# Block sums of the inner rows: made once by VectorE and kept in DRAM scratch instead of summed by GpSimd beside every product

## The chip, the cores and the metric

The kernel runs on one core of one Trainium2 chip. The metric is the device time of the whole program in microseconds (us), as the median of several executions. The five engines are named as the profile names them: PE (TensorE, matrix products), DVE (VectorE), ACT (ScalarE), POOL (GpSimd), and SP (SyncE), which here only issues DMAs, one after the other, in the order of its program.

## The reference, cut to what matters

The reference is one inference step of a two-layer encoder for 1024 prompt tokens and 128 sample tokens, 1152 rows in all. Layer 0 has latent attention and layer 1 a chunked gating mixer. Each is followed by the part that the change is about, a squared-ReLU feed-forward of width 4096 on rows of 1024:

```
def sq_relu_ffn(h, w1, w2):
    return jnp.square(jax.nn.relu(h @ w1)) @ w2

f_p = sq_relu_ffn(modulated_norm(x_p, norm2_g[i], sh2_p, sc2_p), ffn_w1[i], ffn_w2[i])
x_p = x_p + gt2_p[:, None, :] * f_p
```

The matrices are float32. The kernel writes each as hi + lo, two halves that PE can multiply at its fast rate, and makes every product from three (hi·hi, lo·hi, hi·lo): L110, L111 and L112 of the helper `mm3`.

## The kernel before, in words

In each layer the feed-forward has two stages, and both multiply 2x2 blocks with seven products P1 to P7 in place of eight. That needs sums of blocks on both sides: S1, S2, S3, S4 of the one, T1 to T4 of the other.

**The first product** (h @ w1) runs over 16 pairs of 128 hidden channels; a `Pair` is one step. PE makes P1, P5, P6, P2, P7, P4, P3 in this order (`H_ORDER`), each for two groups of tokens. Per pair:
- SP loads the w1 of the next pair (`load_w1`, tiles w0q or w1q by turns).
- POOL makes its four block sums (`w1_sums`).
- ACT and DVE split it: ACT copies the hi half, DVE subtracts for the lo half (`w1_lo_q`, `w1_lo_r`).
- ACT copies P1, P6 and P7 out of PSUM; DVE adds what is left (`read_hidden` C11, C22, C12) into two tiles, piece 0 and piece 1 of 128 x 1152. P3 lies in the PSUM bank of P5, so it waits until C22 has been read.
- DVE squares both pieces (`square`), and SP stores them to the DRAM scratch `hid`.

The 14 pairs between the first and the last are a loop on every engine.

**The second product** (hidden @ w2) runs over 8 slabs of 512 channels, and in each over 4 steps of 256 tokens (32 steps n in a layer), and ends with a product for the sample tokens. In a step PE makes P1, P5, P6, P2, P7, P3, P4. The rows of the hidden matrix come back from DRAM (`load_s`, three tiles by turns, s0, s1, s2). Before the change POOL makes their block sums (`s_sums`: s0q in place, then three into s0r). ACT then copies the hi halves (`s_hi_q`, `s_hi_r`) and DVE subtracts (`s_lo_q`, `s_lo_r`). w2 has its sums and splits on DVE and ACT. ACT copies three products of a step out of PSUM into `tmp`, POOL adds these to the accumulator (`add`), and DVE adds the other four from PSUM (`read`).

Nothing is scheduled by a planner. Each engine runs its rows in the order in which the program is written, with semaphores between them, so one late wait holds up all rows behind it on that engine.

## Time and profile before

| | us |
|---|---|
| median of 3 runs | 2893.41 (2891.55 to 2895.07) |
| the profiled execution, its own time | 2895.44 |
| its span in the trace | 2893.8 |
| PE busy | 2676.5 (92% of the span) |
| DVE busy | 1812.8 (63%) |
| POOL busy | 1183.7 (41%) |
| ACT busy | 1146.9 (40%) |

The busy times are averages over stages with different limits. The first product takes 1000 to 1337 us of the trace in layer 0 and 2145 to 2480 in layer 1, the second product 1340 to 1739 and 2482 to 2883. Ahead of the first product lies the output projection of the mixer, from about 870 and from about 2010. PEclk is the granted TensorE clock, 1.00 for 2.4 GHz and 0.50 for 1.2 GHz.

### The profile page before, as it was taken

Reading aid. Unit: us, or ns where it says so; the run is one execution under the profiler, and the core shown is the slowest. Engines: PE = TensorE matmul, PEld = TensorE weight load, DVE = VectorE, ACT = ScalarE, POOL = GpSimd, SP = SyncE. Lnnn points to the kernel's source line nnn. Section 1 sums busy time; section 2 is a strip of 40 time slices with the busy share of each in tenths; the row PEclk is TensorE's granted clock in tenths of the full one; section 3 lists DMA queues with packets and bytes.
Section 4 is the critical chain, followed back from the end, with each engine's and each line's share of the span. In section 5 each row is a group of like instructions: output and inputs, shape, how many; then the busy total and the mean of one; then the engine's idle time right before and its main releaser. Section 6 shows DMA issues by size and latency. Waiting matters only on the chain.

```text
span 2893.8 us, 45017 instructions
## 1 busy us (share of the span) xinstructions
PE 2676.5 (92%) x16628; PEld 2360.4 (82%) x16628; DVE 1812.8 (63%) x2502; ACT 1146.9 (40%) x2330; POOL 1183.7 (41%) x1022
## 2 busy tenths in 40 slices
PE   6989999899999899999998988999979999998987
PEld 4877878799988799998776766888879999776766
DVE  4577787655566734437888885224673344878886
ACT  3355555345453322224343433223332322444342
POOL 1122102166543322224788871000332222588886
PEclk9999999899999999999999998999999999999999
DMA  6244434322244222233322355125323222432325
GB/s 238 70 163 142 158 109 149 120 67 67 72 147 148 88 93 92 108 108 131 101 85 77 109 146 150 44 66 179 125 79 115 93 92 99 139 102 76 110 77 98
DMA packets 161007, 320.59 MB, mean 111 GB/s; under 512 B 15604, under 2 KB 105876, under 8 KB 157528
## 3 DMA queue, kind: packets, MB, share of 16 engines
q1 hardware_dynamic: 157352, 305.69, 31.6%
q0 software_dynamic: 3504, 12.91, 2.3%
q8 instruction: 92, 1.51, 0.2%
q14 instruction: 59, 0.48, 0.0%
HBM read 249.34 MB, written 69.21 MB: 110 GB/s over the span
## 4 chain that ended last, share of the span: by engine, by line
PE 43%; DVE 15%; issue 7%; POOL 3%; ACT 1%; DMA 1%; SPq 0%; DVEq 0%; POOLq 0%; ACTq 0%
PE psum L110 14%; PE psum L112 14%; PE psum L111 14%; DVE half_acc L3227 3%; DVE half_s0r_lo L3199 1%; DVE half_s1q_lo L3194 1%; DVE half_s_lo L3203 1%; DVE half_s2r_lo L3199 1%; DVE half_s1r_lo L3199 1%; DVE half_s0q_lo L3194 1%; PE psum L3575 0%; DVE half_w1q_lo L3183 0%; DMA gate_w_raw<-in_cm_w_in 0%; DVE half_w2q_lo L3183 0%; DVE half_w0q_lo L3183 0%
## 5 line engine op out<-in xcount | busy, mean ns | idle before, releaser
L2938 POOL TENSOR_TENSOR half_acc<-half_acc,half_tmp 128x512 f32<-128x512 f32 x176 | 309.2, 1810 | 129.7 <-ACT half_tmp L2674 88.8
L2674 ACT ACTIVATE half_tmp<-psum 128x512 f32<-128x512 f32 x176 | 104.4, 593 | 295.5 <-PE psum L112 293.4
L3227 DVE TENSOR_TENSOR half_acc<-half_acc,psum 128x512 f32<-128x512 f32 x240 | 161.4, 678 | 85.0 <-PE psum L112 82.8
L3103 DVE TENSOR_TENSOR half_piece<-psum,half_snap_p 128x576 f32<-128x576 f32 (+1 forms) x34 | 24.5, 721 | 297.9 <-PE psum L112 297.9
L2569 ACT ACTIVATE half_snap_u<-psum 128x288 f32<-128x288 f32 x128 | 52.6, 411 | 282.6 <-PE psum L112 282.6
L110 PE MATMUL psum<-half_h_hi,half_w0q_hi 128*128 128x288 f32 x512 | 154.0, 301 | 6.9 <-DVE half_h_lo L3068 4.5
L111 PE MATMUL psum<-half_h_lo,half_w0q_hi 128*128 128x288 f32 x512 | 152.2, 297 | 0.0
L110 PE MATMUL psum<-half_h_hi,half_w1q_hi 128*128 128x288 f32 x512 | 151.8, 297 | 0.1
L112 PE MATMUL psum<-half_h_hi,half_w0q_lo 128*128 128x288 f32 x512 | 151.7, 296 | 0.0
L111 PE MATMUL psum<-half_h_lo,half_w1q_hi 128*128 128x288 f32 x512 | 151.0, 295 | 0.0
L112 PE MATMUL psum<-half_h_hi,half_w1q_lo 128*128 128x288 f32 x512 | 150.5, 294 | 0.0
L110 PE MATMUL psum<-gate_w_hi,gate_hT_hi 128*128 128x512 f32 x288 | 116.4, 404 | 11.2 <-issue 6.0
L2875 POOL TENSOR_TENSOR half_w0q_raw<-half_w0q_raw 128x512 f32<-128x512 f32 x16 | 20.7, 1295 | 254.2 <-DMA half_w0q_raw<-in_w 254.2
L110 PE MATMUL psum<-half_h_hi,half_w0r_hi 128*128 128x288 f32 x384 | 114.9, 299 | 8.9 <-issue 4.3
L110 PE MATMUL psum<-half_w_hi,half_m_hi 128*128 128x512 f32 x288 | 115.3, 400 | 4.9 <-DVE half_w_lo L1724 3.0
L110 PE MATMUL psum<-half_h_hi,half_w1r_hi 128*128 128x288 f32 x384 | 114.6, 298 | 4.5 <-DVE half_piece L3103 4.5
L2875 POOL TENSOR_TENSOR half_w1q_raw<-half_w1q_raw 128x512 f32<-128x512 f32 x16 | 21.5, 1347 | 236.4 <-DMA half_w1q_raw<-in_w 236.4
L111 PE MATMUL psum<-half_h_lo,half_w1r_hi 128*128 128x288 f32 x384 | 113.9, 297 | 0.0
L111 PE MATMUL psum<-half_h_lo,half_w0r_hi 128*128 128x288 f32 x384 | 113.9, 297 | 0.0
L112 PE MATMUL psum<-gate_w_hi,gate_hT_lo 128*128 128x512 f32 x288 | 113.9, 395 | 0.0
L111 PE MATMUL psum<-gate_w_lo,gate_hT_hi 128*128 128x512 f32 x288 | 113.8, 395 | 0.0
L112 PE MATMUL psum<-half_h_hi,half_w1r_lo 128*128 128x288 f32 x384 | 113.6, 296 | 0.0
(750 smaller groups left out, 9485.0 us busy)
## 6 DMA issues: line engine op xcount, KB each, us to landing
scratch_hid<-half_piece SPq DMA_DIRECT2D x64, 576.0 KB, 3.1
patt_mod_w<-in_ada_w_ffn SPq DMA_DIRECT2D x32, 768.0 KB
half_w0q_raw<-in_w SPq DMA_DIRECT2D x24, 1024.0 KB, 5.8
half_w1q_raw<-in_w SPq DMA_DIRECT2D x24, 1024.0 KB, 5.8
patt_mod_w<-in_ada_w_att SPq DMA_DIRECT2D x16, 1024.0 KB, 5.0
half_s0q_raw<-scratch_hid SPq DMA_DIRECT2D x22, 512.0 KB, 3.7
half_s1q_raw<-scratch_hid SPq DMA_DIRECT2D x22, 512.0 KB, 3.7
half_s2q_raw<-scratch_hid SPq DMA_DIRECT2D x20, 512.0 KB
```

Source lines behind the costliest of these rows:

```text
L110: pe.matmul(out, a_hi, b_hi, start=first, stop=False, skip_group_check=go_on)
L111: pe.matmul(out, a_hi, b_lo, start=False, stop=False, skip_group_check=go_on)
L112: return pe.matmul(out, a_lo, b_hi, start=False, stop=last, skip_group_check=go_on)
L2569: act.activation(out[:, grp, :], psum[:, bank(product, grp), 0:GN], ACT.Copy).then_inc(a.c.snap, 1)
L2674: act.activation(out, psum[:, o_bank_of(product, j), :], ACT.Copy).then_inc(a.c.taken, 1)
L2875: pool.tensor_tensor(q[:, S3, :], q[:, A21, :], q[:, A11, :], ALU.subtract).then_inc(a.c.w1_sum, 1)
L2938: pool.tensor_tensor(part, part, a.tmp[(3 * n + m) % 4][:], ALU.add).then_inc(a.c.added, 1 if i % SLABS else 3)
L3103: dve.tensor_tensor(a.piece[i.par][f_][:, cols, side, :], psum[:, b:b + len(grps), 0:GN], snap[:, cols, :], ALU.add).then_inc(a.c.hid_read, 1)
L3194: dve.tensor_tensor(a.s_qlo[r][:], a.s_q[r][:], f(a.s_qhi[r][:]), ALU.subtract).then_inc(a.c.s_ready, 1)
L3199: dve.tensor_tensor(a.s_rlo[r][:], a.s_r[r][:], f(a.s_rhi[r][:]), ALU.subtract).then_inc(a.c.s_ready, 1)
L3203: dve.tensor_tensor(a.s8_lo[:], a.s8[:], f(a.s8_hi[:]), ALU.subtract).then_inc(a.c.s8_ready, 1)
L3227: dve.tensor_tensor(part, part, of, ALU.add).then_inc(a.c.read, 1)
```

## The change

- DVE makes the block sums of the hidden rows (S3 in place in piece 0, S2, S1, S4, and one for the sample tokens) once per pair, in `block_sums`. SP stores them to new DRAM scratch (`hid_sums`, `hid_8`), and `load_s` and `load_s8` load them beside the rows. `s_sums` and `s8_sum` of POOL are gone.
- The two squares of a pair and its block sums stand at the head of the next pair on DVE (`finish_rows`); those of the last pair stand in the first step of the second product.
- In the second product the sums and splits of the next slab's w2 are placed otherwise over the four steps, on ACT and DVE, and the split of the next rows stands ahead of the read of C11.
- Ahead of the first product the sums and lo halves of h that POOL made (`h_sums`, `h_lo`) go to DVE, and the first pair takes its second group in the same order as its first.
- Where layer 0 ends, the splits of the next weights stand a little earlier.

The diff, cut to its core:

```
@@ -2305,9 +2318,23 @@
                              ).then_inc(a.c.w1_in[par], 16)
 
             def store_piece(a, i, f):
-                sp.wait_ge(a.c.sq_ready, i.count(2, 2 - f))
+                if f == 1:
+                    sp.wait_ge(a.c.sq_ready, i.count(2, 1))
+                else:
+                    sp.wait_ge(a.c.sum_ready, i.count(N_SUM, 1))
                 sp.dma_start(hid[i.index(2, f)], a.piece[i.par][f][:].rearrange("p a b n -> p (a b n)")
                              ).then_inc(a.c.piece_stored[i.par][f], 16)
+
+            def store_sums(a, i):
+                sp.wait_ge(a.c.sum_ready, i.count(N_SUM, N_SUM))
+                for place, s in enumerate((S1, S2, S4)):
+                    sp.dma_start(hid_sums[i.index(1, 0)][:, :, place, :], a.sums[s][:]).then_inc(a.c.sums_stored, 16)
+                sp.dma_start(hid_8[i.index(1, 0)], a.sum8[:]).then_inc(a.c.sums_stored, 16)
+
+            def store_pair(a, i):
+                store_piece(a, i, 1)
+                store_piece(a, i, 0)
+                store_sums(a, i)
 
             def load_w2(a, i, e):
                 u = w2_unit(i, e)
...
@@ -2328,9 +2356,12 @@
                 r = s_place(a, n)[0]
                 sp.dma_start(a.s_q[r][:].rearrange("p e f n -> p (e f) n"),
                              hid_slabs[i % SLABS, :, :, 2 * j * P:2 * (j + 1) * P]).then_inc(a.c.s_in[r], 16)
+                sp.dma_start(a.s_r[r][:].rearrange("p e r n -> p e (r n)"), hid_sum_slabs[i % SLABS, j]
+                             ).then_inc(a.c.s_in[r], 16)
 
             def load_s8(a, i):
                 sp.dma_start(a.s8[:, 0:4, :], hid_slabs[i % SLABS, :, :, SEQ:]).then_inc(a.c.s8_in, 16)
...
@@ -2361,44 +2392,44 @@
                     sp.sem_inc(a.c.piece_stored[1][f], 16)
 
             def hidden_steps(a):
-                store_piece(a, Pair(a, 0), 1)
-                store_piece(a, Pair(a, 0), 0)
+                store_pair(a, Pair(a, 0))
                 with sp.Fori(0, FFS // 2 - 1) as m:
                     for i in (Pair(a, 1, m), Pair(a, 2, m)):
                         sp.wait_ge(a.c.hid_ready, i.count(UNITS))
                         load_w1(a, i, 1)
-                        store_piece(a, i, 1)
-                        store_piece(a, i, 0)
+                        store_pair(a, i)
                 i = Pair(a, FFS - 1)
                 sp.wait_ge(a.c.hid_ready, i.count(UNITS))
                 slab = SLABS * a.layer
                 load_w2(a, slab, 0)
-                sp.wait_ge(a.c.hid_ready, unit_done(i, P5, 1))
+                sp.wait_ge(a.c.hid_ready, unit_done(i, P5, 0))
                 load_w2(a, slab, 1)
                 for n, product in enumerate((P6, P2, P7)):
                     sp.wait_ge(a.c.hid_ready, unit_done(i, product, 1))
                     load_s(a, PAIRS * slab + n)
-                store_piece(a, i, 1)
-                store_piece(a, i, 0)
                 sp.wait_ge(a.c.hid_ready, i.count(UNITS, UNITS))
                 sp.wait_ge(a.c.hid_read, hid_reads(i, 3))
                 load_s8(a, slab)
+                load_w2(a, slab + 1, 0)
+                load_w2(a, slab + 1, 1)
+                store_pair(a, i)
 
             def output_steps(a):
                 for i in slabs_of(a):
                     if i % SLABS:
                         sp.wait_ge(a.c.f_ready, i * N_JOBS)
-                        load_s8(a, i)
-                    if i % SLABS < LAST:
+                    if 0 < i % SLABS < LAST:
                         load_w2(a, i + 1, 0)
                         load_w2(a, i + 1, 1)
-                    else:
+                    if i % SLABS == LAST:
...
@@ -2642,17 +2674,17 @@
                 w2_hi_r(a, i, e)
 
             def s_hi_q(a, n):
-                act.wait_ge(a.c.s_sum, 4 * n + 1)
+                act.wait_ge(a.c.s_in[s_place(a, n)[0]], s_place(a, n)[1])
                 r = s_place(a, n)[0]
                 act.activation(a.s_qhi[r][:], a.s_q[r][:], ACT.Copy).then_inc(a.c.s_hi_ready, 1)
 
             def s_hi_r(a, n):
-                act.wait_ge(a.c.s_sum, 4 * n + 4)
+                act.wait_ge(a.c.s_in[s_place(a, n)[0]], s_place(a, n)[1])
                 r = s_place(a, n)[0]
...
@@ -2879,54 +2915,12 @@
-            def s_sums(a, n):
-                ring, loaded = s_place(a, n)
-                q, r = a.s_q[ring], a.s_r[ring]
-                s1, s2, s4 = (r[:, :, s - 4, :] for s in (S1, S2, S4))
-                x11, x12, x21, x22 = (s_slots(q, s) for s in (A11, A12, A21, A22))
-                pool.wait_ge(a.c.s_in[ring], loaded)
-                pool.tensor_tensor(x21, x21, x11, ALU.subtract).then_inc(a.c.s_sum, 1)
-                pool.wait_ge(a.c.s_sum, 4 * n + 1)
-                pool.tensor_tensor(s2, x21, x22, ALU.add).then_inc(a.c.s_sum, 1)
-                pool.wait_ge(a.c.s_sum, 4 * n + 2)
-                pool.tensor_tensor(s1, s2, x11, ALU.add).then_inc(a.c.s_sum, 1)
-                pool.tensor_tensor(s4, x12, s2, ALU.subtract).then_inc(a.c.s_sum, 1)
-
-            def s8_sum(a, i):
-                pool.wait_ge(a.c.s8_in, 16 * (i + 1))
-                x = a.s8[:, 0:4, :].rearrange("p (e f) n -> p e f n", f=2)
-                pool.tensor_tensor(a.s8[:, 4:6, :], x[:, :, 0, :], x[:, :, 1, :], ALU.add).then_inc(a.c.s8_sum, 1)
...
@@ -2947,22 +2941,12 @@
-                    if n % STEPS + 2 < STEPS:
-                        s_sums(a, n + 2)
-                    if j == 0:
-                        s8_sum(a, i)
...
@@ -3105,36 +3096,53 @@
 
             def square(a, i, f_):
                 if f_ == 1:
-                    dve.wait_ge(a.c.c21_ready, c21_takes(i, 2 if i.first else 1))
-                dve.wait_ge(a.c.hid_read, hid_reads(i, (6 if i.first else 3) if f_ == 0 else (5 if i.first else 2)))
+                    dve.wait_ge(a.c.c21_ready, c21_takes(i, 1))
+                dve.wait_ge(a.c.hid_read, hid_reads(i, 3 if f_ == 0 else 2))
                 x = a.piece[i.par][f_][:]
                 dve.scalar_tensor_tensor(x, x, 0.0, x, ALU.max, ALU.mult).then_inc(a.c.sq_ready, 1)
 
-            def hidden_step(a, i):
+            def block_sums(a, i):
+                dve.wait_ge(a.c.sq_ready, i.count(2, 2))
+                dve.wait_ge(a.c.sums_stored, i.count(64, 1))
+                flat = [a.piece[i.par][f_][:].rearrange("p a b n -> p (a b n)") for f_ in range(2)]
+                x11, x12, x21, x22 = (flat[f_][:, 0:SEQ].rearrange("p (j s n) -> p j s n", s=2, n=P)[:, :, side, :]
+                                      for side in range(2) for f_ in range(2))
+                s1, s2, s4 = (a.sums[s][:] for s in (S1, S2, S4))
+                dve.tensor_tensor(x21, x21, x11, ALU.subtract).then_inc(a.c.sum_ready, 1)
+                dve.wait_ge(a.c.sum_ready, i.count(N_SUM, 1))
+                dve.tensor_tensor(s2, x21, x22, ALU.add).then_inc(a.c.sum_ready, 1)
+                dve.wait_ge(a.c.sum_ready, i.count(N_SUM, 2))
+                dve.tensor_tensor(s1, s2, x11, ALU.add).then_inc(a.c.sum_ready, 1)
+                dve.tensor_tensor(s4, x12, s2, ALU.subtract).then_inc(a.c.sum_ready, 1)
+                dve.tensor_tensor(a.sum8[:], flat[0][:, SEQ:], flat[1][:, SEQ:], ALU.add).then_inc(a.c.sum_ready, 1)
+
+            def finish_rows(a, i):
+                square(a, i, 1)
+                square(a, i, 0)
+                block_sums(a, i)
+
+            def hidden_step(a, i, before):
                 both = (0, 1)
+                finish_rows(a, before)
                 if i.last:
                     slab, n = SLABS * a.layer, STEPS * a.layer
                     w2_sums(a, slab, 0)
                     read_hidden(a, i, C11, both)
                     w2_lo_q(a, slab, 0)
                     read_hidden(a, i, C22, both)
+                    w2_lo_r(a, slab, 0)
                     w2_sums(a, slab, 1)
-                    w2_lo_r(a, slab, 0)
                     s_lo_q(a, n)
                     w2_lo_q(a, slab, 1)
                     read_hidden(a, i, C12, both)
                     s_lo_r(a, n)
                     w2_lo_r(a, slab, 1)
-                    square(a, i, 1)
-                    square(a, i, 0)
                     return
                 read_hidden(a, i, C11, both)
                 w1_lo_q(a, i, 1)
                 read_hidden(a, i, C22, both)
                 w1_lo_r(a, i, 1)
-                square(a, i, 1)
                 read_hidden(a, i, C12, both)
-                square(a, i, 0)
 
             def first_hidden(a):
                 i = Pair(a, 0)
...
@@ -3251,30 +3260,46 @@
                 for n in steps_of(a):
                     i, j = n // PAIRS, n % PAIRS
                     last, more = i % SLABS == LAST, (n + 1) % STEPS > 0
+                    fresh = i % SLABS == 0
+                    if not last and j == (2 if fresh else 1):
+                        w2_lo_q(a, i + 1, 0)
+                    if not last and not fresh and j == 2:
+                        w2_sums(a, i + 1, 1)
+                    if not last and j == 3:
+                        w2_lo_q(a, i + 1, 1)
+                    if fresh and j == 0:
+                        square(a, Pair(a, FFS - 1), 1)
+                        square(a, Pair(a, FFS - 1), 0)
                     read(a, n, C22)
-                    if not last and j >= 2:
-                        w2_lo_q(a, i + 1, j - 2)
+                    if fresh and j == 0:
+                        block_sums(a, Pair(a, FFS - 1))
+                    if more:
+                        s_lo_q(a, n + 1)
                     read(a, n, C11)
                     if more:
-                        s_lo_q(a, n + 1)
+                        s_lo_r(a, n + 1)
+                    if j == 1:
+                        s8_lo(a, i)
+                    if fresh and j == 1:
+                        w2_sums(a, i + 1, 1)
+                    if not last and j == 2:
+                        w2_lo_r(a, i + 1, 0)
                     if last:
                         extra(j, 0)
                     read(a, n, C12)
-                    if more:
-                        s_lo_r(a, n + 1)
+                    if not last and j == 0:
+                        w2_sums(a, i + 1, 0)
                     read(a, n, C21)
-                    if not last and j < 2:
-                        w2_sums(a, i + 1, j)
-                    if not last and j >= 2:
-                        w2_lo_r(a, i + 1, j - 2)
-                    if j == 1:
-                        s8_lo(a, i)
+                    if not last and j == 3:
+                        w2_lo_r(a, i + 1, 1)
                     if last:
+                        extra(j, 1)
                         scale(a, 2 * j)
                         scale(a, 2 * j + 1)
-                        extra(j, 1)
                     if j == PAIRS - 1:
                         read_8(a, i)
+                    if last:
+                        extra(j, 2)
                 scale(a, SAMPLE)
 
             def project_steps(a, start):
```

SP in the loop of the first product, before. Pieces 8448 and 8447 are pieces 1 and 0 of one pair, 8446 and 8445 of the next; `half_w1q_raw<-in_w` is `load_w1`.

```order
L2309 DMA scratch_hid<-half_piece_8447 128x1152
L2368 REGISTER_ALU
L2304 ISA
L2304 DMA half_w1q_raw<-in_w 128x2x1024
L2308 REGISTER_ALU
L2309 ISA
L2309 DMA scratch_hid<-half_piece_8446 128x1152
L2308 REGISTER_ALU
L2309 ISA
L2309 DMA scratch_hid<-half_piece_8445 128x1152
```

The same place in the changed kernel:

```order
L2325 DMA scratch_hid<-half_piece_8447 128x1152
...
L2331 DMA scratch_hid_sums<-half_sum_8449 512x1x128
L2331 ISA
L2331 DMA scratch_hid_sums<-half_sum_8450 512x1x128
L2331 ISA
L2331 DMA scratch_hid_sums<-half_sum_8451 512x1x128
L2332 ISA
L2332 DMA scratch_hid<-half_sum_8452 128x128
L2398 REGISTER_ALU
L2317 ISA
L2317 DMA half_w1q_raw<-in_w 128x2x1024
```

Between the store of piece 0 and the load of w1 stand four stores of sums now, and the first of them waits for the last sum that DVE makes of this pair.

DVE in the same loop, before: the rows from the lo half of one w1 to the reads of C11 and C22 of the pair behind it (L3103 is `read_hidden`, L3111 `square`).

```order
L3089 TENSOR_TENSOR half_w0r_lo<-half_w0r_raw,half_w0r_hi 128x1536
...
L3111 SCALAR_TENSOR_TENSOR half_piece_8448<-half_piece_8448 128x1152
...
L3103 TENSOR_TENSOR half_piece_8447<-psum,half_snap_u_8450 128x2x288
L3111 SCALAR_TENSOR_TENSOR half_piece_8447<-half_piece_8447 128x1152
...
L3103 TENSOR_TENSOR half_piece_8445<-psum,half_snap_p_8449 128x2x288
...
L3084 TENSOR_TENSOR half_w1q_lo<-half_w1q_raw,half_w1q_hi 128x2048
...
L3103 TENSOR_TENSOR half_piece_8446<-psum,half_snap_u_8451 128x2x288
```

The same stretch of the changed kernel (L3094 is `read_hidden`, L3102 `square`, L3111 to L3117 `block_sums`):

```order
L3094 TENSOR_TENSOR half_piece_8447<-psum,half_snap_u_8454 128x2x288
...
L3102 SCALAR_TENSOR_TENSOR half_piece_8448<-half_piece_8448 128x1152
L3102 SCALAR_TENSOR_TENSOR half_piece_8447<-half_piece_8447 128x1152
...
L3111 TENSOR_TENSOR half_piece_8447<-half_piece_8447 128x4x128
...
L3113 TENSOR_TENSOR half_sum_8450<-half_piece_8447,half_piece_8448 128x512
...
L3115 TENSOR_TENSOR half_sum_8449<-half_sum_8450,half_piece_8447 128x512
L3116 TENSOR_TENSOR half_sum_8451<-half_piece_8448,half_sum_8450 128x512
L3117 TENSOR_TENSOR half_sum_8452<-half_piece_8447,half_piece_8448 128x128
...
L3094 TENSOR_TENSOR half_piece_8445<-psum,half_snap_p_8453 128x2x288
...
L3075 TENSOR_TENSOR half_w1q_lo<-half_w1q_raw,half_w1q_hi 128x2048
...
L3094 TENSOR_TENSOR half_piece_8446<-psum,half_snap_u_8455 128x2x288
```

The square of piece 1 moved behind the read of C12, and the sums came in behind both squares. The order of C11, `w1_lo_q` and C22 is as it was.

POOL in the second product, before (L2938 is `add`, L2919 to L2924 `s_sums`):

```order
L2938 TENSOR_TENSOR half_acc_8473<-half_acc_8473,half_tmp_8483 128x512
L2938 TENSOR_TENSOR half_acc_8473<-half_acc_8473,half_tmp_8482 128x512
L2938 TENSOR_TENSOR half_acc_8474<-half_acc_8474,half_tmp_8484 128x512
L2919 TENSOR_TENSOR half_s0q_raw<-half_s0q_raw 128x2x128
L2921 TENSOR_TENSOR half_s0r_raw<-half_s0q_raw 128x2x128
L2923 TENSOR_TENSOR half_s0r_raw<-half_s0r_raw,half_s0q_raw 128x2x128
L2924 TENSOR_TENSOR half_s0r_raw<-half_s0q_raw,half_s0r_raw 128x2x128
```

And in the changed kernel, where L2932 is `add`:

```order
L2932 TENSOR_TENSOR half_acc_8477<-half_acc_8477,half_tmp_8487 128x512
L2932 TENSOR_TENSOR half_acc_8477<-half_acc_8477,half_tmp_8486 128x512
L2932 TENSOR_TENSOR half_acc_8478<-half_acc_8478,half_tmp_8488 128x512
L2932 TENSOR_TENSOR half_acc_8479<-half_acc_8479,half_tmp_8486 128x512
L2932 TENSOR_TENSOR half_acc_8479<-half_acc_8479,half_tmp_8489 128x512
L2932 TENSOR_TENSOR half_acc_8480<-half_acc_8480,half_tmp_8487 128x512
```

Between one step's adds and the next step's nothing is left on POOL.

## Rows read from the trace of the kernel before

**Rows 1.** Busy time by stretch: one pair, one slab; then chain rows three slabs apart.
```profile
1292.40:1314.80 22.40, 22.40 (x170) 22.40 (x169) 9.04 (x7) 6.38 (x10) 5.13 (x4) 1.00 0.28 99
1400.00:1449.80 49.80, 45.03 (x194) 35.54 (x193) 42.20 (x40) 21.23 (x27) 42.43 (x30) 1.00 0.28 90
...
1399.93 1.56 DVE half_s2r_lo L3199
...
1549.36 1.56 DVE half_s2r_lo L3199
```

**Rows 2.** Waits of PE, slab of 1400.0 to 1449.8: waiting line, releaser, total, times, longest.
```profile
PE psum L110 <- ACT half_tmp L2674: 1.7, 2, 1.1
...
PE psum L110 <- DVE half_s1q_lo L3194: 1.4, 1, 1.4
```

**Rows 3.** Groups by line and shape, same slab: busy us, mean ns, idle before.
```profile
L3194 DVE TENSOR_TENSOR half_s2q_lo<-half_s2q_raw,half_s2q_hi 128x1024 fp32r<-128x1024 f32 x1 | 2.3, 2280 | 1.5 <-POOL half_s2r_raw L2924 1.5
...
L3194 DVE TENSOR_TENSOR half_s1q_lo<-half_s1q_raw,half_s1q_hi 128x1024 fp32r<-128x1024 f32 x1 | 1.2, 1212 | 0.0
...
L2938 POOL TENSOR_TENSOR half_acc<-half_acc,half_tmp 128x512 f32<-128x512 f32 x13 | 22.8, 1772 | 6.7 <-DVE half_acc L3227 3.4 <-ACT half_tmp L2674 3.3
L2919 POOL TENSOR_TENSOR half_s0q_raw<-half_s0q_raw 128x256 f32<-128x256 f32 x2 | 3.7, 1853 | 0.0
```

**Rows 4.** Timeline of SP's queue, where one pair ends and the next begins: start, us, line.
```profile
1291.75 3.57 SPq L2309 DMA_DIRECT2D scratch_hid<-half_piece  x2
1295.58 0.41 SPq L2304 DMA_DIRECT2D half_w1q_raw<-in_w  x1
```

**Rows 5.** Timelines of POOL, DVE and PE in the pair from 1292.46 to 1314.86.
```profile
1301.29 1.29 POOL L2875 TENSOR_TENSOR half_w1q_raw<-half_w1q_raw 128x512 f32<-128x512 f32 x1 [16.77 <-DMA half_w1q_raw<-in_w]
...
1292.66 0.76 DVE L3103 TENSOR_TENSOR half_piece<-psum,half_snap_u 128x576 f32<-128x576 f32 x1 [1.08 <-PE psum L112]
1293.45 1.36 DVE L3111 SCALAR_TENSOR_TENSOR half_piece<-half_piece 128x1152 f32<-128x1152 f32 x1
...
1306.70 2.29 DVE L3084 TENSOR_TENSOR half_w1q_lo<-half_w1q_raw,half_w1q_hi 128x2048 fp32r<-128x2048 f32 x1 [0.48 <-POOL half_w1r_raw L2880]
1309.26 0.76 DVE L3103 TENSOR_TENSOR half_piece<-psum,half_snap_u 128x576 f32<-128x576 f32 x1 [0.27 <-ACT half_snap_u L2569]
...
1314.86 0.30 PE L110 MATMUL psum<-half_h_hi,half_w1q_hi 128*128 128x288 f32 x1
```

**Rows 6.** Timeline of DVE: the first and the last of four 128x512 sums in a row.
```profile
1323.89 0.69 DVE L3172 TENSOR_TENSOR half_w0r_raw<-half_w0q_raw 128x512 f32<-128x512 f32 x1 [6.68 <-DMA half_w0q_raw<-in_w]
...
1325.95 0.69 DVE L3177 TENSOR_TENSOR half_w0r_raw<-half_w0q_raw,half_w0r_raw 128x512 f32<-128x512 f32 x1
```

**Rows 7.** Layer 0, second pair: SP, POOL, PE timelines; busy time and clock of a stretch.
```profile
1002.84 0.40 SPq L2304 DMA_DIRECT2D half_w0q_raw<-in_w  x1
...
1010.42 1.31 POOL L2875 TENSOR_TENSOR half_w0q_raw<-half_w0q_raw 128x512 f32<-128x512 f32 x1 [22.73 <-DMA half_w0q_raw<-in_w]
...
1018.86 0.40 PE L110 MATMUL psum<-half_h_hi,half_w1r_hi 128*128 128x288 f32 x1 [2.23 <-DVE half_piece L3103]
...
1023.67 0.29 PE L110 MATMUL psum<-half_h_hi,half_w0q_hi 128*128 128x288 f32 x1
...
1020.00:1023.00 3.00, 3.00 (x15) 3.00 (x14) 1.74 (x2) 0.00 (x0) 0.00 (x0) 0.50 0.11 42
```

**Rows 8.** Layer 1, second pair: timeline of PE, and busy time and clock behind it.
```profile
2163.91 0.40 PE L110 MATMUL psum<-half_h_hi,half_w1r_hi 128*128 128x288 f32 x1 [2.25 <-DVE half_piece L3103]
...
2166.00:2168.00 2.00, 2.00 (x17) 2.00 (x16) 1.38 (x2) 0.00 (x0) 0.00 (x0) 1.00 0.09 37
```

**Rows 9.** DMA issues by line: count, KB each, median us to landing.
```profile
half_w0q_raw<-in_w SPq DMA_DIRECT2D x24, 1024.0 KB, 5.8
...
scratch_x_mid<-half_x SPq DMA_DIRECT2D x9, 512.0 KB, 2.9
...
scratch_mixT<-gate_gT SPq DMA_DIRECT2D x9, 512.0 KB, 3.4
```

195 lines of the change are left out of this document (94 added, 101 removed).

## The prediction

> **What bounds the kernel now.** I read the busy time by stretch first. In a pair of the first product PE is busy for all 22.40 us, with DVE at 9.04, ACT at 6.38 and POOL at 5.13. In a slab of the second product PE is busy 45.03 of 49.80 us, with DVE at 42.20 and POOL at 42.43 [rows 1]. So PE sets the time in the first product, and in the second it idles 4.8 us a slab beside two engines that are 85% full. The chain rows give the slab's length again: the same row stands at 1399.93 and at 1549.36, three slabs in 149.43 us, so 49.8 each [rows 1]. The waits of PE say for whom: for an ACT copy into `tmp` and for the lo half of the next rows, each a few times in the slab [rows 2]. Behind these stands POOL. The 128x1024 lo half takes 2280 ns where POOL's sums run beside it and 1212 ns at its best, and it also idled 1.5 us for a POOL sum; 12 or 13 adds of 128x512 a slab take POOL 1772 ns each, and a 128x256 sum, of half the elements, takes 1853 ns, so its time is not its own work [rows 3]. DVE and POOL slow each other, and both hold up PE. That is the place where the change can gain.
>
> In the first product the slack has to be read along a chain of rows, since the busy times don't show it. Call the start of a pair T, here 1292.46 (22.40 before the first w1 matmul at 1314.86 [rows 5]). DVE reads C12 of the pair before at T+0.2 and squares from T+1.0 [rows 5]. SP stores piece 0 and issues the load of the next w1 at T+3.1 [rows 4]. It has landed when POOL starts its four sums, at T+8.8. The lo half follows at T+14.2, and C22 is read at T+16.8, done at T+17.6 [rows 5]. P3, the last 24 of the pair's 168 matmuls, is due at T+19.2 (22.40 less 24 x 0.133). So the load of w1 may come 1.6 us later than now, no more.
>
> **The change, part by part.**
>
> *The late load of w1.* SP issues it behind `store_pair` now, which waits for DVE's last block sum. From rows: squares start at T+1.0 and two of 1.36 end at T+3.7 [rows 5]. Four 128x512 sums in a row take from 1323.89 to 1326.64, 2.75 us, with POOL idle as here [rows 6]; the fifth is a quarter as wide, 0.2. The sums are done at T+6.6. Before, the load started 0.8 behind the end of the square (1294.81 to 1295.58 [rows 4, 5]) with one store between. With four stores, three more issues of 0.4, it starts at T+8.6, so 5.5 later than now. That is 3.9 more than the slack.
>
> Landing took 5.7 (1295.58 to 1301.29 [rows 4, 5]). Ahead of it in the queue stood one 576 KB store; now it is 832 KB of sums in rows of 512 bytes. At least nothing is added. At most the second pair's landing serves: two pieces just ahead of the load, 1002.84 to 1010.42, 7.6 [rows 7], and a little more for the short rows, 2.5 added. I take 1.0: the store with 512-byte rows lands in 3.4 us against 2.9 for the same 512 KB in long rows [rows 9], so 0.8 for 832 KB, and 0.2 for the larger size. By the Trainium skill ("DMA: Bandwidth & Descriptors", Specifications), rows from 512 bytes up run at line rate. By that 0.8 of it would go, and with 28 pairs the sum would be 22 us lower; the pair of rows 9 speaks against it, but they were not taken beside the same traffic.
>
> The second pair of layer 0 shows what follows a late load, for there it happens already: from POOL's start, 1010.42, to the start of P3, 1018.86, are 8.4 us, and PE idles 2.23 [rows 7]. So now POOL starts at T+15.3 and P3 at T+23.8 in place of T+19.2: PE idles 4.6 us a pair (3.6 to 6.1). P4 will be late as well, since ACT's copies of P7 stand behind its copies of w1; that lies inside the same 4.6.
>
> *The clock behind that wait.* In the second pair of layer 0 the clock falls behind the 2.23 us of idling: 0.50 from 1020 to 1023, and P3 takes 4.8 us (1018.86 to 1023.67) in place of 3.2, 1.6 more [rows 7]. In layer 1 the same pair idles 2.25 and the clock stays at 1.00 [rows 8]. With 4.6 of idling I take the fall as nearly certain and its price as 1.4 on average (0 to 3.2, P3 wholly at 1.2 GHz). A pair then costs 6.0 more than its 22.40.
>
> There are 14 pairs in the loop of each layer. Thirteen pay 6.0: 78 us. The second pair pays 3.9 in layer 0 (2.23 + 1.6) and 2.3 in layer 1 already, so 2.1 and 3.7 are added. Both layers: 156 + 6 = **+162**. In the last pair the first two loads of w2 come 5.5 later by the same queue, and DVE has two squares and five sums more at its head; most is covered by the 22 us of that pair. I put 3 us on each, **+6** (2 to 6 each).
>
> *The second product.* POOL loses four 128x256 sums a step and one a slab; 12 adds are left, about 21 us at today's 1772 ns [rows 3]. DVE's lo halves come back towards 1.2 us, and the hi and lo halves of the next rows wait for a DMA that lands a step ahead, no longer for POOL. The load of sums that each step adds is 384 KB, on DMA engines that are 28% busy [rows 1]. What remains is the order on DVE and ACT: no step of a slab holds more than about 9.5 us of DVE work at unhindered durations, against 9.6 us of PE work (45.03 less the sample product, over four). I expect PE to keep nearly all of it, a slab of 44.8, 5.0 less. Bounds: 6.1 at the most (the five restarts cost a little more than the idle rows show), 3.0 if half the contention with the adds stays. The first slab of a layer takes the last pair's squares and block sums on DVE, 2.7 + 3.0, and I give it nothing. Seven slabs in two layers: **-70** (-42 to -85).
>
> *Ahead of the first product* POOL's 128x1152 sums and lo halves go to DVE, where one takes about 1.3 us. DVE is the fuller engine there, but its own rows lose POOL's hindrance. No row settles it; -4 to +4 a layer, I take **-4** for both. The earlier splits at the end of layer 0 are within 2 us either way, and I take 0.
>
> *The sum.* 162 + 6 - 70 - 4 = +94 on the profiled execution's own 2895.4, which is 2989.4. That execution lies 2.0 above the median of 2893.4, so **2987**.
>
> **The rivals.**
>
> *Faster.* The late load is in the chain as argued, but costs less than the second product gains. The second product and the part ahead give 74, the last pairs take 6; over 28 pairs that is 2.4 us a pair, the point from which it decides. It needs w1 in place at about T+13.1 and a clock that stays up, so a landing of 4.5 us in place of 6.7. For it: piece 0 is stored earlier than before relative to the load, and 512 KB writes land in 2.9. Against it: 1024 KB take 5.8 in the median of 24 loads [rows 9]. At 2.0 us a pair the time is 2893 + 52 - 2 + 6 - 74 = 2875. Chance 0.11. That it comes out even, within 0.2%, 0.04.
>
> *The clock stays at 2.4 GHz*, as in layer 1's second pair [rows 8]. A pair costs 4.6: 26 x 4.6 + 0.7 + 2.3 = 123, and the time is 2893 + 123 + 6 - 74 = 2948. Against it is that the wait is twice as long. Chance 0.16.
>
> *The clock falls for all of P3 in every pair.* Then P3 takes 3.2 more instead of 1.4, a pair 7.8, and the time is 2987 + 27 x 1.8 = 3036. For it are two idle pieces a pair, ahead of P4 and of P3. Chance 0.12. The Trainium skill describes this ("TensorE: Matmul & The Clock Gate", HAM oscillation — how this bites in real kernels): a product that waits in each tile for the next load falls to 1.2 GHz in each tile. By that rule this would be the likeliest case; of this trace's two equal waits [rows 7, 8] one bears it out and one does not.
>
> *The second product gains half*: the waits for POOL go, and in their place PE waits for ACT, which copies w2 halves right behind DVE's sums at the border of two steps. 35 us less gained, 3022. Chance 0.08.
>
> **How the numbers follow.** The likeliest case, as reckoned, has 0.49. Slower: 0.49 + 0.16 + 0.12 + 0.08 = 0.85; same 0.04; faster 0.11. About 0.2%, 6 us, is what a measurement of this kernel can tell from no change. The lowest of the slower cases (3.6 a pair, clock up, 85 gained) is about 2900. Upwards all bounds together give some 3100; I cut at 3050, past the case of 3036. The range 2900 to 3050 leaves out the faster and the even case and a small tail above.
>
> **What would show it.** Right: SP's load of w1 starts some 8.6 us into a pair; POOL's first sum follows near 15; PE waits 3.5 to 6 us a pair for the read of C22; the pair is 26 to 30 us long; the granted clock in the first product drops below 1.00; slabs come down to about 45 with POOL near 20 busy. Wrong: pairs of 22.4 to 24.5 us, or slabs that stay above 48. The prediction fails most easily by the landing time of w1 behind the sum stores and by the clock.

## The result and the profile after

The changed kernel takes 2922.53 us (median of 4 runs, 2918.59 to 2929.64) against 2894.24 in the same session for the kernel before (4 runs, 2891.55 to 2896.59). The ratio is 1.0101, with a 95% interval of 1.0079 to 1.0122: 28 us slower, where the prediction said 94. The direction held, the size was under a third. The profiled execution takes 2918.59 us with a span of 2916.7; it lies 4 us below that median.

Busy time by stretch: start and end, length, then PE, PE's weight loads, DVE, ACT and POOL busy (with instructions), granted clock, DMA share and GB/s. First a pair of the first product, then a slab of the second; they answer to [rows 1].

```profile
1232.21:1260.25 28.04, 24.41 (x171) 23.94 (x170) 11.55 (x12) 6.38 (x10) 5.10 (x4) 0.94 0.32 110
1514.81:1558.76 43.95, 43.85 (x194) 35.98 (x192) 38.26 (x40) 21.19 (x27) 20.28 (x12) 1.00 0.43 141
```

This pair grew from 22.40 to 28.04 us (the mean of 26 is 27.28), 3.6 of it with PE idle, and the clock is below 1.00. The slab shrank from 49.80 to 43.95, and PE is busy in all but 0.1 of it. The trace lists no wait of PE at all in this slab, where [rows 2] had ACT and DVE.

Timelines of SP, DVE, POOL and PE in the pair that starts at T = 1232.21 (start, length, engine, line; in brackets the idle time before and what ended it). They answer to [rows 4, 5].

```profile
1234.60 2.43 SPq L2325 DMA_DIRECT2D scratch_hid<-half_piece  x2
1238.95 2.04 SPq L2331 DMA_DIRECT2D scratch_hid_sums<-half_sum  x3
1241.17 0.50 SPq L2332 DMA_DIRECT2D scratch_hid<-half_sum  x1
1241.94 0.43 SPq L2317 DMA_DIRECT2D half_w1q_raw<-in_w  x1
...
1233.09 2.62 DVE L3102 SCALAR_TENSOR_TENSOR half_piece<-half_piece 128x1152 f32<-128x1152 f32 x2
...
1238.49 0.28 DVE L3117 TENSOR_TENSOR half_sum<-half_piece,half_piece 128x128 f32<-128x128 f32 x1
...
1252.45 2.29 DVE L3075 TENSOR_TENSOR half_w1q_lo<-half_w1q_raw,half_w1q_hi 128x2048 fp32r<-128x2048 f32 x1 [6.48 <-POOL half_w1r_raw L2916]
1254.66 0.75 DVE L3094 TENSOR_TENSOR half_piece<-psum,half_snap_u 128x576 f32<-128x576 f32 x1
...
1247.07 1.29 POOL L2911 TENSOR_TENSOR half_w1q_raw<-half_w1q_raw 128x512 f32<-128x512 f32 x1 [21.29 <-DMA half_w1q_raw<-in_w]
...
1249.80 0.40 PE L110 MATMUL psum<-half_h_hi,half_w0q_hi 128*128 128x288 f32 x1 [1.43 <-ACT half_snap_u L2601]
...
1255.46 0.61 PE L110 MATMUL psum<-half_h_hi,half_w0r_hi 128*128 128x288 f32 x1 [2.20 <-DVE half_piece L3094]
```

The squares start at T+0.9 and the last sum ends at T+6.6. SP's last sum store is issued at T+9.0 and the load of w1 at T+9.7, where it stood at T+3.1. POOL starts at T+14.9, C22 is read at T+22.5, and P3 starts at T+23.25. PE idled twice: 1.43 ahead of P4, 2.20 ahead of P3.

The clock, in busy time by stretch: P3 of this pair, then P4 and P3 of the next pair (1260.25), with the first matmuls of these two.

```profile
1255.40:1260.20 4.80, 4.74 (x24) 4.74 (x25) 1.67 (x2) 0.00 (x0) 0.00 (x0) 0.64 0.00 0
1278.30:1283.40 5.10, 4.96 (x24) 4.75 (x24) 2.33 (x2) 1.87 (x3) 2.56 (x3) 0.67 0.00 0
1284.00:1287.30 3.30, 3.22 (x24) 3.22 (x25) 1.69 (x2) 0.19 (x1) 0.00 (x0) 1.00 0.00 0
...
1278.44 0.40 PE L110 MATMUL psum<-half_h_hi,half_w1q_hi 128*128 128x288 f32 x1 [2.03 <-ACT half_snap_u L2601]
...
1284.08 0.40 PE L110 MATMUL psum<-half_h_hi,half_w1r_hi 128*128 128x288 f32 x1 [0.65 <-DVE half_piece L3094]
```

In the first pair the clock falls in P3, which takes 4.80 us in place of 3.3. In the second it falls in P4 already. P3 couldn't have started before DVE had read C22, so the slower P4 (5.1 us) only shortened the wait for it, from 2.20 to 0.65, and P3 ran at 1.00. This second form costs nothing: from POOL's first sum to P3 are 8.25 to 8.4 us in the pairs whose P4 is slow, and 8.3 to 8.4 in the others.

Groups by line and shape of POOL and DVE in the slab; they answer to [rows 3].

```profile
L2932 POOL TENSOR_TENSOR half_acc<-half_acc,half_tmp 128x512 f32<-128x512 f32 x12 | 20.3, 1703 | 23.7 <-ACT half_tmp L2708 18.0 <-DVE half_acc L3236 5.7
...
L3202 DVE TENSOR_TENSOR half_s2q_lo<-half_s2q_raw,half_s2q_hi 128x1024 fp32r<-128x1024 f32 x2 | 3.5, 1738 | 0.0
...
L3207 DVE TENSOR_TENSOR half_s2r_lo<-half_s2r_raw,half_s2r_hi 128x768 fp32r<-128x768 f32 x2 | 1.9, 944 | 0.0
...
L3202 DVE TENSOR_TENSOR half_s1q_lo<-half_s1q_raw,half_s1q_hi 128x1024 fp32r<-128x1024 f32 x1 | 1.2, 1219 | 0.0
```

Two of DVE's three lo halves shown are still at a mean of 1738 ns against 1219: POOL's adds go on beside them at 1703 ns each. Nobody waits for them now.

Last, the two DMA groups that bear on the landing (count, KB each, median us from issue to landing); [rows 9] had 5.8 for the load.

```profile
half_w0q_raw<-in_w SPq DMA_DIRECT2D x24, 1024.0 KB, 5.3
...
scratch_hid_sums<-half_sum SPq DMA_DIRECT2D x96, 256.0 KB, 2.8
```

Stage by stage, the two profiled executions compare like this (us; a stage is read between the first matmuls of its parts, the second product up to its last matmul):

| part | predicted | measured | how |
|---|---|---|---|
| pairs 3 to 15, both layers | +156 | +127 | 27.32 and 27.24 for 22.40, 13 each |
| second pairs | +6 | +4.5 | 26.5 to 29.3, 25.4 to 27.1 |
| last pairs | +6 | +8.1 | 25.4 to 29.2 and to 29.6 |
| second product | -70 | -90.8 | -45.6 and -45.2 |
| ahead of the first product, with the first pair | -4 | -17.9 | 127.6 to 119.2, 126.2 to 116.7 |
| elsewhere | 0 | -7.8 | 3.9 ahead of 870 us, 3.6 from the end of layer 0's second product through the mixer |

The measured sum is +23.1, from 2895.44 to 2918.59. The last row is not all of one kind. Where layer 0 ends PE waited 2.27 us in the kernel before, and this wait is gone in the changed kernel and in every variant of it, while e3, e4 and e6, which are built on the kernel before, all keep it. That is the work of the earlier splits:

```profile
1745.90 1.09 PE L3546 MATMUL psum<-ident,gate_x 128*128 128x128 f32 x8 [2.27 <-DVE gate_x L3317]
```

The other 5.5 us are code that didn't change. Over all traces of this study the stretch ahead of the output projection of layer 0 ends at 865.6 to 869.6 us, and the mixer of layer 1 takes 268.4 to 272.1, so this part is scatter.

### The profile page after: what moved, and what is told of

It is laid out like the page before. It is cut to its first block, busy times and chain, and to the rows that moved or that the text cites. A ratio compares the mean times of both kernels' runs of the same rounds, so it can differ in the third digit from the quotient of the medians.

```text
span 2916.7 us, 45428 instructions
## 1 busy us (share of the span) xinstructions
PE 2689.7 (92%) x16628; PEld 2387.9 (82%) x16628; DVE 1810.6 (62%) x2672; ACT 1144.7 (39%) x2330; POOL 784.1 (27%) x736
## 4 chain that ended last, share of the span: by engine, by line
PE 30%; issue 28%; POOL 6%; DVE 3%; DMA 2%; SPq 1%; ACT 1%; POOLq 0%; DVEq 0%; ACTq 0%
PE psum L110 10%; PE psum L111 10%; PE psum L112 10%; POOL half_w1r_raw L2913 1%; POOL half_w0r_raw L2915 1%; POOL half_w0r_raw L2913 1%; POOL half_w1q_raw L2911 1%; POOL half_w1r_raw L2916 1%; POOL half_w0q_raw L2911 1%; POOL half_w0r_raw L2916 1%; DMA half_s1r_raw<-scratch_hid_sums 0%; PE psum L3594 0%; SPq L134 0%; DMA half_w1q_raw<-in_w 0%; DVE half_acc L3236 0%
## 5 line engine op out<-in xcount | busy, mean ns | idle before, releaser
L2932 POOL TENSOR_TENSOR half_acc<-half_acc,half_tmp 128x512 f32<-128x512 f32 x174 | 291.5, 1690 | 357.3 <-ACT half_tmp L2708 287.6
L110 PE MATMUL psum<-half_h_hi,half_w1q_hi 128*128 128x288 f32 x512 | 161.5, 315 | 40.5 <-ACT half_snap_u L2601 38.9
L111 PE MATMUL psum<-half_h_lo,half_w1q_hi 128*128 128x288 f32 x512 | 159.3, 311 | 0.0
L112 PE MATMUL psum<-half_h_hi,half_w1q_lo 128*128 128x288 f32 x512 | 158.7, 310 | 0.0
L110 PE MATMUL psum<-half_h_hi,half_w0r_hi 128*128 128x288 f32 x384 | 121.0, 315 | 30.6 <-DVE half_piece L3094 27.2
L110 PEld LDWEIGHTS psum<-half_h_hi,half_w1q_hi 128*128 128x128 f32 x512 | 103.5, 202 | 44.7 <-ACT half_snap_u L2601 42.7
L3094 DVE TENSOR_TENSOR half_piece<-psum,half_snap_p 128x576 f32<-128x576 f32 (+1 forms) x34 | 24.5, 721 | 180.4 <-PE psum L112 180.4
L110 PE MATMUL psum<-half_h_hi,half_w1r_hi 128*128 128x288 f32 x384 | 116.6, 304 | 17.9 <-DVE half_piece L3094 17.9
L110 PE MATMUL psum<-gate_w_hi,gate_hT_hi 128*128 128x512 f32 x288 | 116.6, 405 | 10.0 <-DVE gate_w_lo L3350 5.2
L110 PEld LDWEIGHTS psum<-half_h_hi,half_w0q_hi 128*128 128x128 f32 x512 | 97.8, 191 | 32.7 <-ACT half_snap_u L2601 24.3
L112 PE MATMUL psum<-half_h_hi,half_w0r_lo 128*128 128x288 f32 x384 | 117.8, 307 | 0.0
```

Of the source, the lines that this page charges most:

```text
L110: pe.matmul(out, a_hi, b_hi, start=first, stop=False, skip_group_check=go_on)
L111: pe.matmul(out, a_hi, b_lo, start=False, stop=False, skip_group_check=go_on)
L112: return pe.matmul(out, a_lo, b_hi, start=False, stop=last, skip_group_check=go_on)
L2932: pool.tensor_tensor(part, part, snapshot(a, n, m), ALU.add).then_inc(a.c.added, 1 if i % SLABS else 3)
L3094: dve.tensor_tensor(a.piece[i.par][f_][:, cols, side, :], psum[:, b:b + len(grps), 0:GN], snap[:, cols, :], ALU.add).then_inc(a.c.hid_read, 1)
```

## The experiments

Two questions stood at the start. Theory A: all of the first product's loss comes from where SP's load of w1 stands. Theory B: it comes from DVE's longer head of a pair or from the traffic of the stores. For the slab: did POOL's sums cost by the wait for them, by their load on POOL, or was it the new order (theories C and D)?

**e1: the load first.**

```
-                store_pair(a, Pair(a, 0))
                 with sp.Fori(0, FFS // 2 - 1) as m:
-                    for i in (Pair(a, 1, m), Pair(a, 2, m)):
+                    for i, done in ((Pair(a, 1, m), Pair(a, 0, m)), (Pair(a, 2, m), Pair(a, 1, m))):
                         sp.wait_ge(a.c.hid_ready, i.count(UNITS))
                         load_w1(a, i, 1)
-                        store_pair(a, i)
+                        store_pair(a, done)
...
```

In the last pair of a layer the two loads of w2 likewise go ahead of the stores (cut here).

> The changed kernel, with SP issuing the next load of w1 ahead of the stores of the pair before, in place of behind them; nothing else moves. Theory A (the whole loss of the first product is the place of this load in SP's queue): the load starts at about T+0.2 in place of T+9.7, PE waits for nothing, pairs are 22.4 us again in place of 27.3, and the time falls by 26 x 4.9 + 4.6 = 132 us, to about 2790. Theory B (DVE's longer head of a pair, 11.55 us in place of 9.04, or the sums' stores in the DMA queues hold up the read of C22 or the load whatever the order): pairs stay above 25 us, and the time above 2860.

Measured: 2773.04 us, ratio to the kernel before 0.9589 (0.9573 to 0.9605). Busy time of a pair (T = 1211.16) and of a slab, and SP's timeline in that pair:

```profile
1211.16:1233.56 22.40, 22.40 (x171) 22.40 (x169) 13.83 (x12) 6.38 (x10) 5.61 (x4) 1.00 0.40 138
1499.05:1542.96 43.91, 43.81 (x193) 35.96 (x192) 38.23 (x40) 21.18 (x27) 20.30 (x13) 1.00 0.44 141
...
1211.52 0.42 SPq L2317 DMA_DIRECT2D half_w0q_raw<-in_w  x1
1213.55 2.42 SPq L2325 DMA_DIRECT2D scratch_hid<-half_piece  x2
1220.08 2.06 SPq L2331 DMA_DIRECT2D scratch_hid_sums<-half_sum  x3
```

Same sums, same stores, same DVE rows, and the pair is 22.40 us again with PE busy throughout. DVE is even fuller (13.83 us a pair against 11.55), since POOL's sums now run beside its last two block sums: the fourth takes 1.77 us in place of 0.69, the fifth 1.38 in place of 0.28. Theory A holds and B falls. The time is 17 lower than expected, since second and last pairs recover too: 29.3 and 27.1 to 22.5, 29.2 and 29.6 to 22.9. The first slabs give part of that back, with 49.0 us each in place of 46.2 and 46.8. This version beats both kernels, the one before by 4.1% and the changed one by about 5% (2773.04 / 2922.53, from two sessions).

**e2: a smaller dose.** Both pieces are stored, then the load goes, then the sums (`store_sums(a, done)` behind `load_w1`).

> The changed kernel, with only the four stores of sums behind the next load of w1; both pieces are still stored ahead of it, so it waits for the first block sum. A dose between the two. Theory A with the slack of 1.6 us read from the kernel before: the load starts at about T+5.3, 2.2 later than before the change (T+3.1), PE idles 0.5 to 1 us a pair, clock up, pairs of 22.9 to 23.5, time about 2925 - 26 x 4.1 = 2815. Theory B: pairs above 25 us, since sums and stores are all still there; if the stores that now run beside the load slow its landing (5.1 us in the changed kernel) by over 1 us, pairs of 24.5 or more.

Measured: 2799.51 us, 0.9682 (0.9665 to 0.9698); pairs of 23.2 and 23.1, as theory A had them; the time is 15 below what it said. The load starts at T+5.25 and lands 6.2 later, with a 576 KB store right ahead and the sums' stores beside it. That is the slower landing for which theory B had named pairs of 24.5 or more, and they did not come.

**e3: the kernel before, with nothing but a late load.**

```
-                        sp.wait_ge(a.c.hid_ready, i.count(UNITS))
+                        sp.wait_ge(a.c.hid_ready, i.count(UNITS, (6, 4)[a.layer]))
                         load_w1(a, i, 1)
```

> The kernel before, with only the load of the next w1 made late: in layer 0 it waits for 6 of the pair's 14 units (T+9.6), in layer 1 for 4 (T+6.4). No sums, no new stores, DVE as before. Theory A: layer 0 gets pairs of 26.5 to 28 us as in the changed kernel; layer 1, 3.3 later than before with 1.6 of slack, idles 1.7 and gets pairs of 24 to 24.5 us. Time: 2894 + 13 x 4.9 + 13 x 1.8 + 4 = about 2985. Theory B (the load's place matters little, DVE and stores do): both layers stay below 23.5 us a pair, time below 2920.

Measured: 2971.68 us, 1.0278 (1.0261 to 1.0295). Layer 0 has pairs of 27.37 us, the 27.3 of the changed kernel, without a single sum; layer 1 has 23.47, less than the 24 to 24.5 of theory A, since the load lands in 5.0 us with no store ahead of it, not in the 5.7 of the kernel before. The time is 13 below the 2985 expected. PE's waits in the layer-0 pair from 1268.77 are the two of the changed kernel:

```profile
1286.46 0.40 PE L110 MATMUL psum<-half_h_hi,half_w1q_hi 128*128 128x288 f32 x1 [1.53 <-ACT half_snap_u L2569]
...
1292.11 0.40 PE L110 MATMUL psum<-half_h_hi,half_w1r_hi 128*128 128x288 f32 x1 [2.20 <-DVE half_piece L3103]
```

**e8 and e9: what sets the landing.** e8 stores piece 0 behind the sums. e9 writes the sums in 2 KB rows.

```
             def store_pair(a, i):                       (e8)
                 store_piece(a, i, 1)
-                store_piece(a, i, 0)
                 store_sums(a, i)
+                store_piece(a, i, 0)
```

> The changed kernel, with the 576 KB store of piece 0 moved behind the four stores of sums, so that it stands right ahead of the load of w1; the number of issues ahead of the load is the same, and it starts at about T+9.7 as before. It tests what sets the landing of the load, which the prediction put at 6.7 us and which took 5.1 in the changed kernel, 5.7 in the kernel before (a 576 KB store issued 0.8 us ahead) and 5.1 in layer 0 of the late-load kernel (no store for 6 us ahead). Theory queue (the bytes still under way ahead of it): landing 5.7 to 6.3, pairs 28.0 to 28.5 in place of 27.3, time 2938 to 2953. Rival (landing depends on the load alone): 5.1, pairs of 27.3, time 2918 to 2928.

> The changed kernel, with the three 256 KB stores of sums written in rows of 2 KB in place of 512 bytes; they land in another order in the scratch, so the second product multiplies wrong blocks, at the same cost. The prediction put 0.8 us of landing on the short rows. Theory queue: SP issues these stores 0.7 us apart and the load 1 us behind the last, so they are through in either form; the stores land a little sooner (2.8 to 2.4 us), the load of w1 in 5.0 to 5.1 as now, pairs of 27.2 to 27.4, time 2915 to 2926. Rival (short rows hold up what follows, as priced): landing 4.3 us or the stores' issue faster, pairs 26.5, time 2900 or less.

Measured: e8 2956.37 us, 1.0225 (1.0210 to 1.0241), pairs of 28.4; e9 2916.41, 1.0089 (1.0075 to 1.0103), pairs of 27.2 and 27.1. SP and POOL in a pair of e8:

```profile
1254.89 0.45 SPq L2325 DMA_DIRECT2D scratch_hid<-half_piece  x1
1255.60 0.41 SPq L2317 DMA_DIRECT2D half_w1q_raw<-in_w  x1
...
1261.62 1.27 POOL L2911 TENSOR_TENSOR half_w1q_raw<-half_w1q_raw 128x512 f32<-128x512 f32 x1 [22.88 <-DMA half_w1q_raw<-in_w]
```

From 1255.60 to 1261.62 are 6.0 us, where the pair of the changed kernel shown above has 5.1. In the mean over 26 pairs from issue to POOL's start it is 6.2 against 5.3, and 5.0 to 5.1 in e1 and e3, where no store stands close ahead. So the stores still under way ahead of the load set its landing: a 576 KB store right ahead costs 0.8 to 0.9 over the changed kernel, and the sums' stores, 0.7 us apart, cost 0.2 to 0.3. What was not expected is the issue: at T+10.6 and not at T+9.7, for the store of piece 0, which used to be issued while DVE was still summing, now comes behind the last sum as a fifth issue. It adds 0.7. POOL starts 1.5 us later than in the changed kernel, and the pair is only 1.1 longer, since the clock fell in 22 of 26 pairs but each time in P4, ahead of the longer wait. P4 and P3 of the pair from 1245.18:

```profile
1264.30:1269.90 5.60, 4.98 (x24) 4.73 (x24) 2.95 (x3) 2.32 (x3) 2.52 (x2) 0.70 0.00 0
1269.90:1273.30 3.40, 3.33 (x25) 3.33 (x26) 1.68 (x2) 0.09 (x1) 0.00 (x0) 1.00 0.00 0
```

So the pair of 28.4 fits the theory partly by luck: a later issue made it longer and a clock that cost nothing made it shorter. The time lies 3 us above what was expected. The DMA groups of e9:

```profile
half_w0q_raw<-in_w SPq DMA_DIRECT2D x24, 1024.0 KB, 5.2
...
scratch_hid_sums<-half_sum SPq DMA_DIRECT2D x96, 256.0 KB, 2.2
```

With long rows the stores land in 2.2 in place of 2.8, and SP's issue of three takes 1.4 us in place of 2.0, so the load starts 0.85 earlier; the landing itself is unchanged. The faster issue is what the rival named as one of its ways, with pairs of 26.5; the theory's time came out, and its pairs within 0.1, though not for its reason. Neither had what followed: the pair gained only 0.1. P3 starts 0.8 earlier (T+22.8 and 22.6 against 23.6) but takes 4.45 us in place of 3.7 in the mean, because the clock now falls in P3 in 20 of 26 pairs (P3 over 4 us), against 7 in the changed kernel.

The doses together, each a mean over 13 or 26 pairs read from the timelines, in the order of POOL's start:

| kernel | load issued | POOL starts | pair | pairs with the clock below 0.99 |
|---|---|---|---|---|
| e1 | T+0.35 | T+5.4 | 22.40 | 0 of 26 |
| before | T+3.25 | T+9.2 | 22.40 | 0 of 26 |
| e2 | T+5.25 | T+11.5 | 23.15 | 0 of 26 |
| e3, layer 1 | T+6.8 | T+11.8 | 23.47 | 0 of 13 |
| e9 | T+9.05 | T+14.35 | 27.15 | 21 of 26 |
| e3, layer 0 | T+9.95 | T+15.0 | 27.37 | 6 of 13 |
| changed | T+9.9 | T+15.25 | 27.28 | 16 of 26 |
| e8 | T+10.6 | T+16.75 | 28.38 | 22 of 26 |

Where the clock falls goes with the idle time ahead of P4. In the 65 pairs of the last four rows in which it fell, the 32 falls in P4 stand behind idle times of 1.79 to 3.62 us, and the 33 falls in P3 behind 0.49 to 1.97 ahead of P4. The mean idle time ahead of P4 is 0.92 in e9, 1.81 in the changed kernel and 3.30 in e8, and P3 takes 4.45, 3.70 and 3.29. This was read from the finished runs and not tested by one of its own, and it doesn't say in which pairs the clock stays up: those have 0.66 to 3.62.

**e4 and e6: the slab without POOL's sums, and with idle ones.** e4 is the kernel before without `s_sums`; the second load per step brings the bytes of the changed kernel. e6 adds, to e4, four sums a step that nobody waits for, and e5 adds the same to e1:

```
+            def idle_sums(a, n):                        (e5, e6)
...
+                for _ in range(4):
+                    a.idle_n += 1
+                    pool.wait_ge(a.idle_done, a.idle_n)
+                    pool.tensor_tensor(a.idle[:], a.idle[:], a.idle[:], ALU.subtract).then_inc(a.idle_done, 1)
```

> The kernel before, but POOL's four block sums a step are left out and the tile that they filled is loaded from the hidden rows instead, with the bytes of the changed kernel; so this second product multiplies wrong blocks in the sums' place, at the same cost, and its time is read for the slabs alone. The order of DVE and ACT is that of before. Theory C (POOL's sums are the whole cost of a slab, by waits or by contention): slabs of 43.9 to 44.3 us as in the changed kernel, time 2894 - 16 x 5.7 = about 2803. Rival D (the new order of w2's sums and splits over the steps gives part of it): slabs of 45.5 to 48, time 2830 to 2870.

> The kernel before without POOL's block sums (e4, slabs of 45.2), with the same idle sums put back on POOL; as in e4 the second product multiplies wrong blocks at the same cost. It splits the 4.6 us that a slab gained there. Theory contention: slabs of 48.5 to 49.8, time about 2822 + 14 x 4 = 2878. Theory wait: slabs of 45.2 to 46.5, time 2822 to 2840. I hold contention for the larger part here, since before's order leaves the splits of a step no room.

> The kernel with the load first (e1, 2773 us, slabs of 43.9), with four idle sums of 128x256 a step added on POOL at the place where its block sums stood before, from the second slab on, on a tile that nobody else reads; the rows of the second product don't wait for them. Theory contention (DVE and POOL slow each other, and that alone held PE up): slabs go back above 47 us, time above 2773 + 14 x 3 = 2815. Theory wait (PE's rows stood behind POOL's sums; the load on POOL itself costs little, since DVE has 5.7 us of slack a slab): slabs stay within 43.9 to 45, time 2773 to 2790. POOL busy comes back to about 42 of a slab if the adds slow again.

Measured: e4 2821.80 us, 0.9763 (0.9746 to 0.9781); e6 2847.53, 0.9842 (0.9826 to 0.9859); e5 2800.24, 0.9681 (0.9665 to 0.9697). One slab of each, e4, e6, e5, in busy time by stretch:

```profile
1511.15:1556.35 45.20, 44.17 (x193) 35.80 (x192) 37.49 (x40) 21.18 (x27) 23.52 (x14) 1.00 0.41 134
```

```profile
1518.13:1564.82 46.69, 44.43 (x193) 35.78 (x192) 40.05 (x39) 21.18 (x27) 40.98 (x30) 1.00 0.39 130
```

```profile
1504.36:1550.29 45.93, 44.39 (x193) 35.80 (x192) 40.28 (x39) 21.20 (x27) 38.03 (x29) 1.00 0.42 135
```

Before's slab is 49.8. With POOL as busy but nobody waiting for its sums it is 46.7, so the wait was worth 3.1. Without the load it is 45.2: the load was worth 1.5. What is left by subtraction, 1.3, to 43.9, I put down to the new order of DVE and ACT; no run changes the order alone. So e4 lies between its two theories: rival D had a part, but the slab is 0.3 and the time 8 below its ranges. In e6 I had held contention for the larger part; it is half of the wait, and the slab is 0.2 above the range of the wait theory. e5 lies between its two theories: with the new order the load on POOL costs 2.0 (45.9), a bit over the 45 that I allowed the wait theory. e4 also ends the last pair at 22.9 us in place of 25.4: there PE had waited 2.8 us for a lo half of DVE (`s_lo_q`) that stood behind POOL's first sums of the second product.

**e7: the sums and two lo halves of h back on POOL**, on top of e1 (`h_sums` and `h_lo` of the first group of tokens as in the kernel before, PE waiting for POOL in two products of the first pair).

> The kernel with the load first (e1), with the four sums and two lo halves of h ahead of the first product put back on POOL; the order of the first pair on PE stays that of the changed kernel. Theory: before, the 6.2 us of POOL's lo halves stretched DVE's scale and shift rows of the last prompt tile from 1.2 to 3.5 us each, and PE waited 4.5 us for them; so the first product starts about 5.5 us later in each layer than in e1 and the time rises by 8 to 12 us, to about 2783. Rival (the gain lay in the order of the first pair): the first product starts where it does in e1, within 1 us, and the time stays at 2773 to 2776.

Measured: 2785.38 us, 0.9638 (0.9618 to 0.9657), 12 above e1. From the first transpose of the output projection to the second pair are 126.0 us in layer 0 and 123.5 in layer 1, against 119.1 and 116.6 in e1: 6.9 in each layer, of the 8.4 and 9.5 that the change gained there. The first product starts 5.5 and 5.8 us later, as expected. The remaining 1.5 and 2.6 belong to what e7 leaves as it is, the order of the first pair and the lo half of the second group; no run splits them. DVE's scale and shift of the last prompt tile, and POOL beside them:

```profile
950.05 3.72 DVE L3063 SCALAR_TENSOR_TENSOR half_h<-half_x,half_small,half_scale_t 128x1024 f32<-128x1024 f32 x1 [0.71 <-POOL half_small L2897]
953.80 3.51 DVE L3066 TENSOR_TENSOR half_h<-half_h,half_shift_t 128x1024 f32<-128x1024 f32 x1
...
949.98 6.25 POOL L2935 TENSOR_TENSOR half_h_lo<-half_h_raw,half_h_hi 128x1152 fp32r<-128x1152 f32 x2
```

The rows of the kernel before that should have been read for this are the same ones, DVE, POOL and then PE:

```profile
951.56 3.70 DVE L3056 SCALAR_TENSOR_TENSOR half_h<-half_x,half_small,half_scale_t 128x1024 f32<-128x1024 f32 x1 [2.13 <-POOL half_small L2860]
955.29 3.51 DVE L3059 TENSOR_TENSOR half_h<-half_h,half_shift_t 128x1024 f32<-128x1024 f32 x1
...
951.49 6.24 POOL L2903 TENSOR_TENSOR half_h_lo<-half_h_raw,half_h_hi 128x1152 fp32r<-128x1152 f32 x2
...
958.86 1.97 PE L3414 MATMUL psum<-ident,half_h 128*128 128x128 f32 x8 [4.51 <-DVE half_h L3059]
```

and DVE in the changed kernel:

```profile
943.60 1.28 DVE L3036 SCALAR_TENSOR_TENSOR half_h<-half_x,half_small,half_scale_t 128x1024 f32<-128x1024 f32 x1 [0.72 <-POOL half_small L2896]
944.92 1.23 DVE L3039 TENSOR_TENSOR half_h<-half_h,half_shift_t 128x1024 f32<-128x1024 f32 x1
```

A row of 1.28 us takes 3.70 while POOL's lo halves run, the next 3.51 in place of 1.23, and PE waits 4.51 for the second; in the changed kernel that wait is 0.9. The Trainium skill ("SBUF — State Buffer", Who interferes with whom) says that a DVE row with two SBUF inputs contends with a GpSimd row that reads SBUF, over a pair of ports that they share under an exclusive lock. The trace agrees in kind. If the lock held for one whole row of POOL, the DVE row would take POOL's 3.1 us and its own 1.28, an estimate of 4.4, and it takes 3.70.

## Why the prediction was right in direction and wrong in size

The mechanism was right: the late load makes every pair wait, the slabs gain less than that costs, and the time rises. What failed are three terms of the sum, each too high: the clock's price in a pair (1.4 us put, 0.5 measured), the second product (-70 put, -90.8 measured) and the part ahead of the first product (-4 put, -17.9 measured).

- **The late load: right at its end, by luck on the way.** Issue at T+8.6 predicted, T+9.9 in the mean; POOL at T+15.3 predicted, T+15.25 in the mean; P3 at T+23.8 predicted, T+23.6 measured. Two errors cancelled. SP's sum stores stand 0.7 us apart and not 0.4, so the load left 1.3 later. The landing took 5.1 to 5.4 and not 6.7: I added 1.0 for the stores ahead and should have taken some off, since the 576 KB store had passed by then (e8 puts it back and gets 6.2 in the mean). The 0.8 for short rows was charged to the wrong place (e9): they slow SP's issue, not the load behind. The rule on row size of the Trainium skill ("DMA: Bandwidth & Descriptors", Specifications), line rate from 512 bytes up, fits the landing of the load and not the stores themselves (2.8 against 2.2 us).
- **The slack of 1.6: nearly right.** POOL may start at about T+10.4 by it. e2 at T+11.5 loses 0.75 and e3's layer 1 at T+11.8 loses 1.07, so the edge is near T+10.7.
- **The clock's price: the step that failed in the first product.** "With 4.6 of idling I take the fall as nearly certain and its price as 1.4 on average." The clock fell in 16 of 26 pairs, but in 9 of these it fell in P4, ahead of the second wait, where it is free. P3 takes 3.70 in the mean in place of the 3.2 + 1.4 of the sum, so the price was 0.5. Of the 29 us missed in the loop, 0.9 us a pair (23) is this and the rest the earlier start of P3. Pairs with the fall in P4 are 27.1 us long in the mean, those without a fall 26.9, those with it in P3 28.1. The idle time ahead of P4 goes with the place of the fall (the table's four late kernels); what decides whether it falls at all is open. The rival of a clock that stays up came nearer in time, 2948, with 4.6 for a pair where 4.88 was measured, though its premise was wrong: the clock did fall.
- **The rival of full fall.** The rule of the Trainium skill ("TensorE: Matmul & The Clock Gate", HAM oscillation — how this bites in real kernels) would have the clock fall in each pair, as a product that waits in each tile falls in each. The traces bear it out in 16, 21 and 22 of 26 pairs and in 6 of 13 of e3's layer 0, at idle times of 3 to 4 us a pair in the mean, and in none of the 39 of e2 and e3's layer 1, at 0 to 1.0. My rival priced every fall at the full 3.2 us; a fall in P4 costs nothing.
- **The second product: 21 too little.** The term was -70 and measured -90.8. I put the floor of a slab at 44.8 and 43.9 is reached: PE's busy time itself fell by 1.2. The likely reason is that a restart behind a wait counts as busy: pairs of the changed kernel with two waits and the clock at 1.00 show 22.92 us busy in place of 22.40. I had taken 45.03 less little for the floor. And I gave the first slab of a layer nothing, while it gained 4.4 and 3.6; the seven behind it gained 5.9 each. The reading of where the gain lies (PE behind POOL's sums) was right. That the lo halves would come back to 1.2 us was not, and did not matter.
- **Ahead of the first product: 14 too little.** "No row settles it" was wrong: rows of the kernel before settle the larger part of it, 4.51 us of PE waiting behind two stretched DVE rows (0.9 are left after the change), and e7 gives back 6.9 in each layer. Weighing DVE's total load against POOL's was the mistake.
- **The last pairs** cost 8.1 for 6. e1 shows their parts: 6.3 and 6.7 by the late loads of w2, less 2.5 each gained where POOL's first sums went (e4). As e1's first slabs are 2.9 and 2.2 longer, the late loads cost 3.4 and 4.5 over both.
- **The earlier splits** at the end of layer 0, put at 0 and within 2 us, took away a wait of 2.27 us.

The three large errors all made the kernel look slower: 29, 21 and 14 us, of 71 in all. The remaining 7 are the second and last pairs (-1 together), the earlier splits (2) and the scatter of unchanged stages (5 to 6).

## What to carry to other kernels

A new store that waits for late work must not stand ahead of a load on the same in-order queue: here moving the loads of weights ahead of it turned 1% slower into 4.1% faster, at no other change. When a clock fall is priced, ask first which product the fall slows, and whether a wait behind it absorbs it. And where an engine's row takes three times its best duration, look at what runs beside it before judging by how full the engines are.

## What the runs showed of the hardware that I had not expected

- Three stores of 256 KB in 512-byte rows take SP 2.04 us, in 2 KB rows 1.38, and each lands in 2.8 against 2.2 us.
- A 1024 KB load lands in 5.0 us with no store close ahead (e1, e3) and in 6.1 right behind a 576 KB store (e8), means of 26 pairs.
- Starting P3 0.8 us earlier bought 0.1 (e9), since the clock then fell in P3 in 20 of 26 pairs in place of 7. With more idle time ahead of P4 (e8) it fell in P4 in 22 of 26, and P3 kept its 3.29 us.
- DVE and POOL cost each other far more in some rows (1.28 to 3.70 us) than in others: the 128x1024 lo halves have a mean of 1738 ns beside POOL's adds, against 1219.
